# Full-width block-diagonal products in rounds five to eight of the recurrence's chunk stages

## The reference

```
for each direction, each chunk of 32 tokens, each head:
    factor = (inverse of the two 16x16 diagonal blocks)
    F1      = factor @ [keys | raw products]
    coupled = factor @ (off @ F1)            # off: the 16x16 block off the diagonal
    Ftil    = coupled + F1
    G       = raw @ Ftil  (+ keys, + raw products)
    per chunk: state' = tm @ state + rm      # tm, rm from G, Ftil, values and keys
```

## Time and profile before

| | |
|---|---|
| median of 3 runs | 2351.34 us (2348.07 to 2355.38) |
| the profiled execution | 2351.12 us, span 2349.3 us |
| TensorE busy | 1780.6 us, 76% of the span |
| VectorE, ScalarE, GpSimd busy | 823.6, 649.5, 218.6 us |
| HBM read | 584.99 MB |
| rc0, chunk stage | 866 to 911 us |
| rc1, chunk stage | 933 to 976 us |
| rl0, chunk stage | 1122 to 1168 us |
| rl1, chunk stage | 1193 to 1241 us |

### The profile page before, as it was taken

The page is one execution under the profiler, slowest core; times in us unless marked ns, Lnnn a source line. Parts: engine busy times, 40 slices in busy tenths (PEclk is TensorE's granted clock), DMA queues, the critical chain, the costliest instruction groups (busy, mean ns, idle before and its releaser), DMA issues. The chain is left out here.

```text
span 2349.3 us, 38529 instructions
## 1 busy us (share of the span) xinstructions
PE 1780.6 (76%) x16973; PEld 1203.5 (51%) x16973; DVE 823.6 (35%) x1175; ACT 649.5 (28%) x1055; POOL 218.6 (9%) x206
## 2 busy tenths in 40 slices
PE   6999988988999877698778977666565556656565
PEld 6997987867778665597667852111111111111111
DVE  4654445765554564477464542000000000000001
ACT  4434445554333354334442330000000000000001
POOL 0100014420121032001330000000000000000000
PEclk9999998999999987799886988777778887787877
DMA  6654642336986410061003459999999999999997
GB/s 207 198 180 146 196 154 72 95 135 220 314 284 215 157 47 3 14 191 59 4 3 96 143 214 391 427 428 428 428 428 428 428 428 428 428 428 428 428 428 298
DMA packets 178562, 588.74 MB, mean 251 GB/s; under 512 B 8131, under 2 KB 141326, under 8 KB 153822
## 3 DMA queue, kind: packets, MB, share of 16 engines
q1 hardware_dynamic: 177026, 585.38, 64.6%
q10 hardware_dynamic: 1372, 0.92, 0.2%
HBM read 584.99 MB, written 1.28 MB: 250 GB/s over the span
## 5 line engine op out<-in xcount | busy, mean ns | idle before, releaser
L3376 PE MATMUL ps<-ex_ring,ex_xe 128*32 128x512 f32 x1440 | 236.0, 790 | 159.1 <-DMA ex_ring<-in_exp_w 159.1
L3449 DVE TENSOR_TENSOR ex_hid<-ps,ex_silu 128x512 f32<-128x512 f32 x16 | 11.1, 692 | 866.4 <-PE ps L3376 866.4
L3376 PEld LDWEIGHTS ps<-ex_ring,ex_xe 128*32 128x32 f32 x1440 | 45.2, 127 | 343.7 <-DMA ex_ring<-in_exp_w 251.7
L209 PE MATMUL ps<-xt_hi,ffn_whi 128*128 128x256 f32 x704 | 204.1, 290 | 7.6 <-DVE xt_lo L372 7.6
L210 PE MATMUL ps<-xt_lo,ffn_whi 128*128 128x256 f32 x704 | 200.0, 284 | 0.0
L211 PE MATMUL ps<-xt_hi,ffn_wlo 128*128 128x256 f32 x704 | 199.8, 284 | 0.0
L181 DVE TENSOR_TENSOR ffn_wlo<-ring,ffn_whi 128x2048 fp32r<-128x2048 f32 x66 | 154.3, 2338 | 113.6 <-ACT ffn_whi L174 113.2
L3398 PE MATMUL ps<-ex_ring,ex_ht 128*32 128x512 f32 x688 | 118.3, 822 | 72.4 <-DMA ex_ring<-in_exp_w 67.7
L174 ACT CAST ffn_whi<-ring 128x2048 fp32r<-128x2048 f32 x66 | 125.2, 1901 | 112.2 <-PE ps L211 96.9
L209 PEld LDWEIGHTS ps<-xt_hi,ffn_whi 128*128 128x128 f32 x704 | 136.8, 194 | 17.3 <-issue 16.3
L210 PEld LDWEIGHTS ps<-xt_lo,ffn_whi 128*128 128x128 f32 x704 | 136.3, 194 | 1.2 <-issue 1.2
(11 more groups left out here) (772 smaller groups left out, 3956.2 us busy)
## 6 DMA issues: line engine op xcount, KB each, us to landing
ex_ring<-in_exp_w SPq DMA_DIRECT2D x133, 2048.0 KB, 46.1
ring<-in_exp_w SPq DMA_DIRECT2D x40, 2048.0 KB, 46.0
ring<-in_w_in SPq DMA_DIRECT2D x55, 1024.0 KB, 5.2
ex_late<-in_exp_w SPq DMA_DIRECT2D x19, 2048.0 KB, 46.1
ring<-in_ffn_w_gate SPq DMA_DIRECT2D x22, 1024.0 KB, 6.3
ring<-in_ffn_w_up SPq DMA_DIRECT2D x22, 1024.0 KB, 5.4
ring<-in_ffn_w_down SPq DMA_DIRECT2D x22, 1024.0 KB, 4.9
ffn_mod_tile<-in_mod_w SPq DMA_DIRECT2D x12, 1024.0 KB, 7.2
```

What stands on the lines that cost most here:

```text
L209: nc.tensor.matmul(out, lhs[0], rhs[0], start=start, stop=False, skip_group_check=shared)
L3376: mm = mm_(ps[32 * q:32 * q + 32, 4 + u, :], xe[:, k], w[:, 512 * q:512 * q + 512], start=k == 0, stop=k == KC - 1)
L3449: v.tensor_tensor(hid[:], ps[:, 5, :], silu[:], ALU.mult).then_inc(S["hid"], 1)
```

## The change

Rounds 5 to 8 use 128x128 block-diagonal weights. Of each quarter and round, the 16 small products become 4 (one per head), and their weights are the spread matrices: the factor in `spread(q)[:, 0]` (rounds 5 and 7), off and then raw in `spread(q)[:, 1]` (rounds 6 and 8). The factor's spreading in round 4 takes the place of ScalarE's plain copy, by the same means as in rounds 1 to 3. GpSimd spreads off and raw by a product with a mask, `blocks`. As `both` is then taken, the right sides move: `ftil` into the place of `bk`, `pair` into that of `ar`, `coupled` into a buffer of its own. Minus the identity in `pair` is written by GpSimd instead of ScalarE.

```
@@ buffers
-        pair = sb("pair", [P, NQ, 2, 4, CH])
+        later = sb("later", [P, NQ, 12 * CH])
-        RAW, SPREAD, FLIPPED, TWO, LOW3, FTIL, KM = 1, 2, 4, 6, 7, 8, 9
+        RAW, SPREAD, FLIPPED, TWO, LOW3, FACTOR, FTIL, KM = 1, 2, 4, 6, 7, 8, 9, 10
         def coupled(q):
-            return by_heads(both[:, q, P:P + 4 * wide])
+            return by_heads(later[:, q, 0:4 * wide])
         def ftil(q):
-            return by_heads(both[:, q, 4 * P:4 * P + 4 * wide])
+            t, h4 = its[q]
+            return bk.rearrange("p c j t -> p (c j) t")[:, 4 * h4:4 * h4 + 4, P * t:P * t + wide]
+        def pair(q):
+            t, h4 = its[q]
+            return ar[:, 2 * h4:2 * h4 + 2, 0, P * t:P * t + P]
         def spread_places(q, r):
-            first, k0, n = {1: (0, 0, 8), 2: (P, 0, 8), 3: (P, 1, 4)}[r]
+            first, k0, n = {1: (0, 0, 8), 2: (P, 0, 8), 3: (P, 1, 4), 4: (0, 0, 4)}[r]
@@ tensor
-            def by_chunks(out, hs, left, right):
-                for c in range(4):
-                    mm = mm_(out[group(c), wide * hs:wide * hs + wide], left[group(c)], right[group(c)], start=True, stop=True)
+            def by_heads_of(out, left, right):
+                for hs in range(4):
+                    mm = mm_(out[:, wide * hs:wide * hs + wide], left[:, hs], right(hs), start=True, stop=True)
                 return mm
                 elif r == 5:
-                    pe.wait_ge(by_act, FACTOR)
+                    pe.wait_ge(by_dve, FACTOR)
+                    pe.wait_ge(by_act, FACTOR_HIGH)
...
+                    mm = by_heads_of(out, spread(q)[:, 0],
+                                     lambda hs: tok[:, 1, t, head_columns(h4, hs)] if ctx_only else f1(q)[:, hs])
                 elif r == 6:
+                    pe.wait_ge(S["off_spread"], q + 1)
                     pe.wait_ge(by_act, F1)
+                    mm = by_heads_of(out, spread(q)[:, 1], lambda hs: f1(q)[:, hs])
                 elif r == 7:
                     pe.wait_ge(by_act, COUPLED)
+                    mm = by_heads_of(out, spread(q)[:, 0], lambda hs: coupled(q)[:, hs])
                 elif r == 8:
+                    pe.wait_ge(S["raw_spread"], q + 1)
                     pe.wait_ge(by_dve, FTIL)
+                    mm = by_heads_of(out, spread(q)[:, 1], lambda hs: ftil(q)[:, hs])
@@ scalar
-            nc.scalar.activation(pair[:, :, 1], eye.unsqueeze(1).unsqueeze(1).to_broadcast([P, NQ, 4, CH]), ACT.Copy, scale=-1.0
-                                 ).then_inc(S["minus"], 1)
-                elif r <= 3:
+                elif r <= 4:
                     packed, places = spread_places(q, r)
                     for c in (2, 3):
                         ins = nc.scalar.copy(places[group(c), :, c], packed[group(c)])
-                elif r == 4:
-                    ins = nc.scalar.copy(both[:, q, 0:P], bank(q, r)[:, 0:P])
@@ gpsimd
             def expand(q):
                 pool.wait_ge(S[f"by_dve{q}"], RAW)
+                added = pair(q).rearrange("p k (h j) -> p k h j", h=4)
+                tt(added[:, 0], raw[:, q, :, 0:CH], eye.unsqueeze(1).to_broadcast([P, 4, CH]), ALU.add)
+                nc.gpsimd.tensor_scalar(added[:, 1], eye.unsqueeze(1).to_broadcast([P, 4, CH]), -1.0, None, ALU.mult
+                                        ).then_inc(S["expanded"], 1)
...
+            def blocks(out, x):
+                return tt(out.rearrange("p h (c j) -> p h c j", c=4), x.unsqueeze(2).to_broadcast([P, 4, 4, CH]),
+                          g.blkmask[:].rearrange("p (c j) -> p c j", c=4).unsqueeze(1).to_broadcast([P, 4, 4, CH]), ALU.mult)
+            for q in range(NQ):
+                pool.wait_ge(S[f"pe{q}"], 5)
+                pool.wait_ge(S[f"by_act{q}"], KEPT)
+                blocks(spread(q)[:, 1], off[:, q]).then_inc(S["off_spread"], 1)
+            for q in range(NQ):
+                pool.wait_ge(S[f"pe{q}"], 7)
+                blocks(spread(q)[:, 1], raw[:, q, :, CH:2 * CH]).then_inc(S["raw_spread"], 1)
@@ vector
-                if r in (4, 5, 6, 9, 10, 11):
+                if r in (5, 6, 9, 10, 11):
                     continue
-                elif r == 3:
+                elif r in (3, 4):
                     ins = spread_low(q, r)
```

More of the change, by code:

```diff
@@ L2535, in recurrence_chunks @@
         front = sb("front", [P, NQ, 12 * CH])
-        pair = sb("pair", [P, NQ, 2, 4, CH])
+        later = sb("later", [P, NQ, 12 * CH])
         eye = g.pat[:, 0:CH]
-        RAW, SPREAD, FLIPPED, TWO, LOW3, FTIL, KM = 1, 2, 4, 6, 7, 8, 9
+        RAW, SPREAD, FLIPPED, TWO, LOW3, FACTOR, FTIL, KM = 1, 2, 4, 6, 7, 8, 9, 10
         G2 = KM if ctx_only else KM + 1
-        KEPT, HIGH, YT3, FACTOR, F1, COUPLED, RM = 2, 3, 6, 7, 8, 9, 10
+        KEPT, HIGH, YT3, FACTOR_HIGH, F1, COUPLED, RM = 2, 3, 6, 7, 8, 9, 10
         block = ctx.enter_context(nc.Block(no_gpsimd_drain=True))
@@ L2549, in spread @@
             return both[:, q].rearrange("p (k h n) -> p k h n", k=2, h=4)
-        def factor(q):
-            return by_heads(both[:, q, 0:P])
         def coupled(q):
-            return by_heads(both[:, q, P:P + 4 * wide])
+            return by_heads(later[:, q, 0:4 * wide])
         def ftil(q):
-            return by_heads(both[:, q, 4 * P:4 * P + 4 * wide])
+            t, h4 = its[q]
+            return bk.rearrange("p c j t -> p (c j) t")[:, 4 * h4:4 * h4 + 4, P * t:P * t + wide]
         def flipped(q):
@@ L2564, in f1 @@
             return by_heads(front[:, q, 0:4 * wide])
+        def pair(q):
+            t, h4 = its[q]
+            return ar[:, 2 * h4:2 * h4 + 2, 0, P * t:P * t + P]
         def yt3(q):
-            return pair[:, q, 0]
+            return pair(q)[:, 0].rearrange("p (c j) -> p c j", c=4)
         def g2c(q):
-            return pair[:, q, 1]
+            return pair(q)[:, 1].rearrange("p (h j) -> p h j", h=4)
         def order():
@@ L2657, in _ @@
                     pe.wait_ge(by_act, HIGH + 1)
-                    y2, b4 = pair[:, q, 0], pair[:, q, 1]
+                    y2, b4 = (pair(q)[:, k].rearrange("p (h j) -> p h j", h=4) for k in range(2))
                     for hs in range(4):
@@ L2670, in _ @@
                 elif r == 5:
-                    pe.wait_ge(by_act, FACTOR)
+                    pe.wait_ge(by_dve, FACTOR)
+                    pe.wait_ge(by_act, FACTOR_HIGH)
                     if not ctx_only:
                         pe.wait_ge(S["joined"], q + 1)
-                    for hs in range(4):
-                        right = tok[:, 1, t, head_columns(h4, hs)] if ctx_only else f1(q)[:, hs]
-                        mm = by_chunks(out, hs, factor(q)[:, hs], right)
+                    mm = by_heads_of(out, spread(q)[:, 0],
+                                     lambda hs: tok[:, 1, t, head_columns(h4, hs)] if ctx_only else f1(q)[:, hs])
                 elif r == 6:
+                    pe.wait_ge(S["off_spread"], q + 1)
                     pe.wait_ge(by_act, F1)
-                    for hs in range(4):
-                        mm = by_chunks(out, hs, off[:, q, hs], f1(q)[:, hs])
+                    mm = by_heads_of(out, spread(q)[:, 1], lambda hs: f1(q)[:, hs])
                 elif r == 7:
                     pe.wait_ge(by_act, COUPLED)
-                    for hs in range(4):
-                        mm = by_chunks(out, hs, factor(q)[:, hs], coupled(q)[:, hs])
+                    mm = by_heads_of(out, spread(q)[:, 0], lambda hs: coupled(q)[:, hs])
                 elif r == 8:
+                    pe.wait_ge(S["raw_spread"], q + 1)
                     pe.wait_ge(by_dve, FTIL)
-                    for hs in range(4):
-                        mm = by_chunks(out, hs, raw[:, q, hs, CH:2 * CH], ftil(q)[:, hs])
+                    mm = by_heads_of(out, spread(q)[:, 1], lambda hs: ftil(q)[:, hs])
                 else:
@@ L2734, in _ @@
                         act.wait_ge(S[f"by_dve{q}"], LOW3)
-                        ins = nc.scalar.copy(yt3(q).rearrange("p c j -> p (c j)"), bank(q, r)[:, 0:P])
-                elif r == 4:
-                    ins = nc.scalar.copy(both[:, q, 0:P], bank(q, r)[:, 0:P])
+                        ins = nc.scalar.copy(pair(q)[:, 0], bank(q, r)[:, 0:P])
                 elif r == 5:
@@ L2740, in _ @@
                 elif r == 6:
-                    ins = nc.scalar.copy(both[:, q, P:P + 4 * wide], bank(q, r)[:, 0:4 * wide])
+                    ins = nc.scalar.copy(later[:, q, 0:4 * wide], bank(q, r)[:, 0:4 * wide])
                 else:
@@ L2754, in expand @@
                 pool.wait_ge(S[f"by_dve{q}"], RAW)
-                tt(pair[:, q, 0], raw[:, q, :, 0:CH], eye.unsqueeze(1).to_broadcast([P, 4, CH]), ALU.add
-                   ).then_inc(S["expanded"], 1)
+                added = pair(q).rearrange("p k (h j) -> p k h j", h=4)
+                tt(added[:, 0], raw[:, q, :, 0:CH], eye.unsqueeze(1).to_broadcast([P, 4, CH]), ALU.add)
```

(9 more changed lines are left out.)

## The result

The changed kernel is slower: 2364.76 us median of 4 executions (2358.66 to 2376.50) against 2349.80 of before (2348.07 to 2355.38), a ratio of 1.0062 with a 95% interval of 1.0036 to 1.0088. In 12 further executions its median was 2359.74 against 2349.51 (ratio on record 1.0028, interval 1.0011 to 1.0045; the two medians alone give 1.0044). So it is slower by 0.3 to 0.6%, and neither interval reaches 1. The forecast was 2348.9, with a range of 2338 to 2358.

What follows compares the result with a forecast made beforehand. TensorE's stream was taken to bound rounds 5 to 8, waiting for instruction pages, one per 3.7 to 4.0 us. Rounds 5 to 8 with spreading +2.2, moved page boundaries -4.4: -2.2 on 2351.12 gives 2348.9 us, range 2338 to 2358.

Steps and rivals of the forecast that it cites:

- Pace of a full-width matmul: Rounds 5 to 8: a matmul with a 128x128 weight costs 0.114 us, set by the weight load; bounds 0.100 and 0.148.
- Round 4 to 5: Spreading the factor in round 4 starts round 5 about 0.25 us later, 1.0 us over four phases.
- Rounds 5 to 8 in sum: Rounds 5 to 8 of all four phases go from 57.2 to 58.4 us, without the later start of round 5.
- Rounds 9 to 12: Instruction-page boundaries move, so rounds 9 to 12 gain 1.1 us a phase, -4.4 us; bounds nothing and -8.
- GpSimd's cover: GpSimd's eight spreading products per phase, 1.26 us each, finish before rounds 6 and 8 need them and cost nothing.
- part 1: Rounds 5 to 8: 32 full-width matmuls a round at 2.4 GHz, 3.65 us a round, 58.4 us over four phases.
- Rival B: Clock falls to 1.2 GHz in rounds 5 to 8: 3.1 us more a round, 2374 for rc0 and rc1; chance 0.07.
- the case of the forecast: The whole kernel at 2348.9 us, its own range 2344 to 2354; chance 0.50.

Runs made afterwards that it cites:

- dup_rc1: The changed kernel with each product of rounds 5 to 8 in the context phases streaming its 64 columns twice; 2347.10 us median of 12, ratio to before 0.9989.
- again1: The changed kernel again with no edit, in 12 new executions; 2359.74 us median against 2349.51 of before, ratio on record 1.0028.
- small_all1: The changed kernel with rounds 5 to 8 multiplying 32x32 diagonal blocks one by one, as before the change; 2354.12 us median of 10, ratio 1.0023.
- narrow_rla: The changed kernel with 64 instead of 96 columns in rounds 5 to 8 of the latent phases; 2368.58 us median of 5, ratio 1.0049.
- small_rca: The changed kernel with 32x32 products in the context phases, full-width weights in the latent phases alone; 2352.59 us median of 12, ratio 1.0021.

## Why the prediction was wrong

- **Pace of a full-width matmul**: taken 0.114, measured 0.112 (32 in 3.57 us) at the full clock. Right, with its reason: 64, 96 and 128 columns cost the same.
- **Round 4 to 5**: 0.25 us forecast. The distance from round 4's start to round 5's went from 2.87 or 2.88 to between 3.02 and 3.08, so 0.15 to 0.2. Right.
- **Rounds 5 to 8 in sum**: three phases at 14.4 would make 57.7 for four, +0.5 against the 57.18 of before, where +1.2 was forecast. Right.
- **Rounds 9 to 12**: -4.4 forecast, -5.8 measured, with the bound at -8. The term was undersized. In rc0, of the 2.00 us gained, 0.74 are gaps that went (1.05 before, 0.31 now); for the rest I point to the clock, which now stayed up there (0.93 against 0.50 in rc0, 0.93 against 0.68 in rl0, 0.82 against 0.64 in rl1) and which the sum did not count.
- **GpSimd's cover**: right. In rounds 5 to 8 of the changed kernel PE never waited for it; off was spread from 1151.4 on in rl0, with round 6 at some 1156.6.
- **The step that failed** is one sentence of part 1: "The new products keep the whole array busy without a gap, so I cost them at 2.4 GHz." A PE that is busy by the trace was taken for one that keeps its clock. The 0.90 and 0.87 of the earlier trace rows were means, too: already in the kernel before the clock fell ahead of round 9, at 898.9 us in rc0 and 963.7 in rc1. In rc1 the new rounds began at the full clock and lost it 0.7 us later, and being busy without a gap did not bring it back: at 213 ns a matmul it stayed at 1.2 GHz from 949.9 us to the end of the phase. The small products before waited for instruction pages, which by my reading leaves little for a slow clock to cost; the new ones pay in full. Rival B had the price of a round (3.1 us, measured 3.26) and its reason, a loaded weight used for just 64 columns, which `dup_rc1` bears out: with 128 columns rc1 kept its clock. It had a chance of 0.07 and let both context phases fall. One phase of four was enough. By stretches: rounds 5 to 8 +12.9 (rc1 +11.65, rl0 +1.3, rl1 +0.9, rc0 -1.0), rounds 9 to 12 -5.8, round 4 to 5 +0.7, in sum +7.8; the two profiled executions differ by 7.54 (2358.66 less 2351.12).
- With the clock up the sum comes to +0.5 + 0.7 - 5.8 = -4.6 us, an estimate from these rows: 2345 against a median of 2349.5. The two quickest executions of `again1`, 2343.3 and 2345.5, lie there. By the times, the case of the forecast came about in two of sixteen executions; the median belongs to B's mechanism, in one phase.

**What stays open.** What makes rc1's clock fall where rc0's holds, with nearly the same stream, was not settled. The traces show one difference: round 5 began 10.6 us after a rise of the clock in rc0 and 23 us after one in rc1. The runs show that either doubled columns or a filled round 4 takes the slow executions away; by which way the second does it is open, since in its profile the clock had fallen and risen again between the two edited rounds. Putting `again1`'s stream at another distance from a rise was not tried. And a second step of 9 us occurs in kernels of several kinds: the state sweep behind rl0. Its line, in `again1` (21.3 us) and in `dup_rc1` (12.4 us):

```profile
L2876 PE MATMUL ps<-vtok,rl_g x32: 421/421/474, 1181.9 to 1203.2; 128*128 128x64 f32 x32
```

```profile
L2880 PE MATMUL ps<-vtok,rl_g x32: 274/276/473, 1175.3 to 1187.7; 128*128 128x64 f32 x32
```

In `small_all1` and `narrow_rla` it took 21.3 us too. Single executions of before reach 2366 us, so its clock may fall there as well, which no profile shows; whether the change makes it more likely (`small_all1` and `small_rca` lie 3 to 5 us over before) was not tried apart.

## What to carry to other kernels

Before products are merged to fill the array, ask what bounds the small ones: here it was, by the best reading of the gaps, the supply of instructions, and halving their number with 64x64 weights gained 22 us. 128x128 weights made the weight load the bound, at 0.112 us a matmul for 64, 96 or 128 columns. Price such a stage at both clocks, even if it leaves TensorE no gap: in rc1 of three profiles a stage bound by weight loads, with 64 moving columns, lost the clock and did not get it back. Columns streamed twice, or a repeated product in a gap, can be cheaper than none.

## What was not expected of the hardware

- The same fp32 matmul with a 128x128 weight took 275 or 421 ns and came every 0.112 or 0.213 us, by the granted clock alone. In rc1 this went on for 26 us of unbroken TensorE work at a granted clock of 0.50; being busy did not bring the clock back.
- 128 moving columns in place of 64 cost 0.05 us in 14.4, and the changed kernel's median fell by 12.6 us with them.
- The rule of the Trainium skill ("TensorE: Matmul & The Clock Gate", What's actually happening) that sustained matmuls bring the full clock does not hold in rc1: 122 matmuls back to back, from 950.2 to 976.05 us, stayed at 1.2 GHz.
